# ScalarE copies the turned tile ahead of its exponentials, and two one-number activations stand where tables are to come in

## What is computed

```python
def diff_attention(q, k, v, lam):
    ...
        s = jnp.einsum("bhcqd,bhckd->bhcqk", qb, kf) * (dh ** -0.5)
        a = jax.nn.softmax(s, axis=-1)
        return jnp.einsum("bhqk,bhkd->bhqd", a[:, :, 0] - lam * a[:, :, 1], vf)
def mixer_c(...):
    o = diff_attention(q, k, v, lam)
    o = rms_norm(o, subln, LN_EPS) * (1.0 - lambda_init)
    return o.reshape(B, S, C_MIX).astype(x.dtype) @ w_out
```

## Time and profile before

| | us |
|---|---|
| median of 3 runs | 2598.41 |
| lowest, highest | 2597.32, 2599.71 |
| the profiled execution, its own time | 2594.23 |
| its span (first to last instruction) | 2592.4 |
| TensorE busy in the span | 2473.3 (95%) |
| VectorE busy | 1169.7 (45%) |
| ScalarE busy | 688.6 (27%) |
| GpSimd busy | 1898.8 (73%) |
| mean granted clock of TensorE | 0.979 |

### The profile page before, as it was taken

The page is one execution under the profiler, slowest core; times in us unless marked ns, Lnnn a source line. Parts: engine busy times, 40 slices in busy tenths (PEclk is TensorE's granted clock), DMA queues, the critical chain, the costliest instruction groups (busy, mean ns, idle before and its releaser), DMA issues.

```text
span 2592.4 us, 32309 instructions
## 1 busy us (share of the span) xinstructions
PE 2473.3 (95%) x11170; PEld 1897.2 (73%) x11170; DVE 1169.7 (45%) x1541; ACT 688.6 (27%) x1244; POOL 1898.8 (73%) x1537
## 2 busy tenths in 40 slices
PE   7988989999989989999999999999999999999998
PEld 6745668888867853668888777866888878678886
DVE  7485463331061677463330176445423565553323
ACT  2264333330021138133330023145110131450101
POOL 8803368888867953678888778844999898449996
PEclk9989999999999999999999999899999999999999
DMA  4201012222212210112222223211222222112222
GB/s 170 89 1 41 33 65 98 96 97 97 98 63 94 94 51 1 61 66 96 94 96 97 89 72 107 86 58 41 98 98 97 89 98 81 49 50 101 93 97 90
DMA packets 57544, 207.08 MB, mean 80 GB/s; under 512 B 6512, under 2 KB 6896, under 8 KB 57200
## 3 DMA queue, kind: packets, MB, share of 16 engines
q1 hardware_dynamic: 55872, 199.87, 21.9%
q10 hardware_dynamic: 1584, 5.96, 0.6%
HBM read 203.71 MB, written 2.10 MB: 79 GB/s over the span
## 4 chain that ended last, share of the span: by engine, by line
PE 79%; DVE 11%; POOL 4%; issue 3%; ACT 2%; DMA 0%; POOLq 0%; DVEq 0%; ACTq 0%; SPq 0%
PE bank L696 22%; PE bank L697 21%; PE bank L698 21%; PE bank L771 3%; PE bank L726 3%; POOL w_hi L2322 2%; PE bank L820 2%; PE bank L799 2%; POOL w_lo L2325 2%; DVE region L1754 1%; PE bank L885 1%; DVE branch_lo L1734 1%; DVE moving_lo L1959 1%; PE bank L841 1%; DVE x L1968 1%
## 5 line engine op out<-in xcount | busy, mean ns | idle before, releaser
L2322 POOL TENSOR_TENSOR w_hi<-ring,unit 128x512 fp32r<-128x512 f32 x750 | 843.6, 1125 | 554.6 <-PE bank L698 417.1
L2325 POOL TENSOR_TENSOR w_lo<-ring,w_hi 128x512 fp32r<-128x512 f32 x750 | 1032.8, 1377 | 58.8
L696 PE MATMUL bank<-moving_hi,w_hi 128*128 128x512 f32 x1962 | 777.8, 396 | 29.9 <-DVE moving_lo L1959 18.8
L697 PE MATMUL bank<-moving_lo,w_hi 128*128 128x512 f32 x1962 | 771.6, 393 | 0.0
L698 PE MATMUL bank<-moving_hi,w_lo 128*128 128x512 f32 x1962 | 770.4, 393 | 0.0
L696 PEld LDWEIGHTS bank<-moving_hi,w_hi 128*128 128x128 f32 x1962 | 372.0, 190 | 125.0 <-issue 25.8
L698 PEld LDWEIGHTS bank<-moving_hi,w_lo 128*128 128x128 f32 x1962 | 372.6, 190 | 78.9
L697 PEld LDWEIGHTS bank<-moving_lo,w_hi 128*128 128x128 f32 x1962 | 372.6, 190 | 76.7 <-issue 1.2
L2269 DVE TENSOR_TENSOR region<-region,bank 128x512 f32<-128x512 f32 x64 | 39.7, 681 | 278.4 <-PE bank L698 278.4
L1941 DVE SCALAR_TENSOR_TENSOR region<-x,bank 128x512 f32<-128x512 f32 x32 | 21.3, 686 | 284.6 <-PE bank L698 284.5
L771 PE MATMUL bank<-region 64*128 64x512 f32 (+3 forms) x448 | 130.5, 601 | 15.6 <-DVE region L1728 4.4
(11 more groups left out here) (271 smaller groups left out, 3477.4 us busy)
## 6 DMA issues: line engine op xcount, KB each, us to landing
ring<-in_weights SPq DMA_DIRECT2D x375, 512.0 KB, 3.2
x<-in_x_t ACTq DMA_DIRECT2D x4, 512.0 KB, 8.4
out<-region SPq DMA_DIRECT2D x8, 256.0 KB, 2.2
region<-in_tables ACTq DMA_DIRECT2D x1, 1312.0 KB, 6.6
region<-in_tables ACTq DMA_DIRECT2D x1, 1024.0 KB, 5.6
region<-in_p_t ACTq DMA_DIRECT2D x2, 512.0 KB, 4.8
region<-in_tables SPq DMA_DIRECT2D x1, 320.0 KB, 10.1
small_w<-in_small_w ACTq DMA_DIRECT2D x1, 320.0 KB, 6.0
```

Of the source, the lines that this page charges most:

```text
L696: pe.matmul(bank, lhs[0], rhs[0], start=start, stop=False, skip_group_check=True)
L697: pe.matmul(bank, lhs[0], rhs[1], start=False, stop=False, skip_group_check=True)
L2322: pool.tensor_tensor(w_parts[0][:, s, at], ring[:, s, at], unit[:, 0:1].broadcast_to([P, BLK // 2]), ALU.mult).then_inc(split_hi, 1)
L2325: pool.tensor_tensor(w_parts[1][:, s, at], ring[:, s, at], w_parts[0][:, s, at].bitcast(F32), ALU.subtract).then_inc(split_ready, 1)
```

## The change

Three edits in ScalarE's `attention_c`. The copy of turn n-3 is issued ahead of the two exponentials of turn n instead of behind them. An exponential of one number for each partition (the constant of the layer norm) is issued ahead of the loop, and a root of the same number behind the loop, ahead of the last three copies; both write to `table_in`, a new tile of two numbers that nobody reads. The new tile lies behind `unit`, so the tiles allocated after it move by its size.

```diff
         unit = sb("unit", [P, 1])
+        table_in = sb("table_in", [P, 2])
...
+                act.activation(table_in[:, 0:1], col("eps_ln"), ACT.Exp)
                 for n, (u, i) in enumerate(turns):
                     t = TURN_AT[(u, i)]
                     act.wait_ge(turned, max(t - 2, first_c))
+                    if n >= 3:
+                        copy_turned(*turns[n - 3])
                     for c in range(2):
                         act.wait_ge(maxed, 2 * t + c + 1)
                         at = 2 * (t % 4) + c
                         act.activation(blend_slot(t, c), psum[2 * (t % 2) + c], ACT.Exp, bias=negmax[:, at:at + 1],
                                        accum_out=rowsum[:, at:at + 1]).then_inc(exped, 1)
-                    if n >= 3:
-                        copy_turned(*turns[n - 3])
                     if i == 3 and n > 2 * ST:
                         finish(units[n // ST - 2])
+                act.activation(table_in[:, 1:2], col("eps_ln"), ACT.Sqrt)
                 for at in turns[-3:]:
                     copy_turned(*at)
```

## The result

| | before | after |
|---|---|---|
| median of 6 runs | 2598.26 | 2587.41 us |
| lowest, highest | 2597.26, 2599.71 | 2586.96, 2591.98 us |
| profiled execution, its span | 2594.23, 2592.4 | 2587.32, 2585.5 us |

The ratio of after to before is 0.9961, with a 95% interval from 0.9948 to 0.9974. The change gains 10.9 us between the medians and 6.9 between the profiled executions. The forecast was 6.0 (a ratio of 0.9977, above that interval); the stage came out nearly as worked, and the whole did not. The two profiled executions also differ where nothing was changed: the stage starts at 945.10 before and at 942.80 after, so of their 6.9 us 2.3 lie ahead of it, and 1.9 are lost again behind it. What the change does to the stage is therefore read from distances inside it.

The account below looks back on a forecast made before the run. TensorE, holding 79% of the span, was taken as the bound, with stalls and two table loads on its path in the subtracted softmaxes. 1.28 + 3.48 + 1.28 = 6.04 us takes 2598.41 to 2592.4; range 2590.2 to 2595.8.

Parts of the forecast that it names:

- Step 1: Start of the subtracted softmaxes: the added exponential moves its table load into ScalarE's idle time; gain 1.28 us, hidden price 0.
- the clock's 0.5 to 0.6: Second scores: less TensorE standing may keep the clock up, 0.60 us more, total 6.6; kept inside the forecast's 0.74.
- Step 2: Softmax loop: copy ahead of exponentials removes the 0.58 us stall of each unit's first value matmul; gain 3.48 us.
- Six stalls, not seven: Seven value matmuls waited for the copy, the last after the last scores; six count, 6 x 0.58 = 3.48 us.
- The exponentials late by ScalarE at a unit's border: Behind finish and copy, exponentials start 0.43 us late; 0.64 us of slack remains, so the cost is 0.
- Step 3: End of the softmaxes: the root added ahead of the last three copies takes its table load off the chain; gain 1.28 us.
- the last turning was not late: The copy it needs, delayed by the added root, would still end in time, with 0.29 us to spare.
- Squares brought no other load: Copies and squares run under the root's table; squares needing another table would bring the load back, but they don't.
- A load costs more than its bar: Rival: each load also holds up its surroundings, making the tables worth double; 8.7 us in total, 2589.7, chance 0.02.
- The stage's 6.04: Forecast gain in the subtracted softmaxes of heads_c: 1.28 + 3.48 + 1.28 = 6.04 us.
- the shift passes on unchanged: Everything after the softmaxes waits through TensorE, so the full gain reaches the end: median 2598.41 becomes 2592.4 us.
- dips of the clock behind the stage: Later clock dips, lying in time and not in the program, hit busier or idler TensorE: up to 1 us either way.

Follow-up runs that it names:

- e3: Kernel before plus both added activations (early exponential and early root) with their tile, copy order unchanged: ratio 0.9982, stage 94.71 us.
- e4: Kernel before plus only the early added exponential with its tile, no added root, copy order unchanged: ratio 0.9993, stage 96.06 us.
- e7: Kernel before with only the copy of each unit's last turn moved ahead of the exponentials, no added activation: loop 60.21 us against 63.96.
- e8: Kernel before with the other three of four copies moved ahead, each unit's last turn's copy left behind the exponentials: loop 63.96 us.
- e6: Kernel before plus only the early added root with its tile: ratio 0.9992, stage 96.40 us.
- e15: Kernel before, unchanged, one more profiled execution: stage 97.39 us, span 2593.8 us.
- e1: Kernel before, unchanged, profiled once more: ratio 1.0001, stage 97.85 us, span 2591.7 us.
- e11: Changed kernel without its early exponential (order and root only): ratio 0.9970, stage 94.18 us.
- e13: Changed kernel without its early root (order and exponential only): ratio 0.9961, stage 92.62 us.
- e14: Changed kernel, run a third time unchanged: ratio 0.9959, stage 91.24 us.
- e9: Kernel before plus six unread 128 x 512 matmuls after the sums of squares, in TensorE's gap ahead of the roots: ratio 1.0003.

## Why the prediction was wrong

1. *Step 1, the exponential's table.* Right in place and direction. The load lies in the idle time (936.59), the second scores start 5.01 us after the first (942.80, 947.81) in place of 6.29, exactly the 1.28. What I left to a rival, the clock's 0.5 to 0.6, came in e3 and e4 whole (against the first profile of before) and in the changed kernel for about 0.1; against the mean of the four profiles of before, for nothing.

2. *Step 2, the order.* Right, and e7 and e8 show the cause alone. Six stalls, not seven, were on the path. The term was 3.48 and measured 3.75: five boundaries give 0.59 each, the first gives 0.78, since the next maxima there come 2.56 us behind the last ones instead of 3.34. The exponentials late by ScalarE at a unit's border (984.76) cost nothing, as worked; they were late by 0.26 us, and not by 0.43. From the first scores to the last value matmul the stage is 5.1 us shorter (6.49 - 1.36) where 4.8 was forecast.

3. *Step 3, the root's table.* Right: 1.36 for 1.28, and the last turning was not late. The copy that the last turning needs started at 1025.94 and was done by 1026.5, 0.8 us ahead of that turning (1027.32), where I had worked out 0.29. Squares brought no other load.

4. *A load costs more than its bar.* That rival is out: hiding the root's load gained 1.36 us (e6), its bar's 1.28 and 0.08, and the stage gained 6.5 and not 8.7. The Trainium skill (ScalarE: Activation LUTs, "What ACT_TABLE_LOAD costs") would have had 2.66 for a switch; the traces here don't agree.

5. *The sum and the range.* Here the prediction failed. The stage's 6.04 measured 6.49 (91.35 against 97.84). Put on the 2598.41 that I started from, that is 2591.9, inside the range; the measured 2587.41 is 4.5 lower. The failed step is the sentence that the shift passes on unchanged from the profiled execution to the median, with a spread of 1.2 us. Its three runs did not show how executions of this kernel spread. Over all comparisons, 101 executions of before have a mean of 2597.1 and a standard deviation of 2.5 us, 19 of the changed kernel 2588.3 and 1.5. Those means are 8.85 apart. So of the 10.9 us, 6.3 are the stage's in the mean of the profiles (6.5 in the first two); 8.85 - 6.3 = 2.5 are the change's too, in the means, and not in the stage; and 10.85 - 8.85 = 2.0 are the luck of six executions against six (1.1 by those of before lying above their mean, 0.9 by those of after below theirs). The comparisons were not all made on one chip, and taken one by one they give 10.1, 9.1, 10.0 and, with five executions only, 7.6; weighted by their executions 9.4, which would leave 1.4 to luck.

6. *What the 2.5 are.* The clock on record with each execution gives about half. Its mean over the span is 0.9776 in the 95 executions of before that have it and 0.9787 in the 19 of the changed kernel, and among executions with the same recorded clock (0.977 to 0.980, to three digits) the two kernels are 7.0 to 8.1 us apart, 7.5 by a fit over all. So some 1.3 us go with a lower clock in the executions of before. About 0.4 of this is the clock behind the gap ahead of the roots (e15 against e1). I had written of it in the wrong direction: dips of the clock behind the stage were noise to me, up to 1 us either way, lying in time and not in the program, while the gap of step 3 itself has a part in one of them, and others move with the program (the low stretch at 1112 to 1118 of before, 0.53, stands at 1104 to 1110 of the changed kernel, 0.50). For the rest, 7.5 - 6.3 = 1.2, I have no cause that the runs show; with a standard error of 0.4 on the 7.5 and on the 8.85 alike, it is uncertain by about 0.8, and it stays open. The parts measured over the whole (order 2.6 to 3.3, exponential 1.2 to 1.4, root 2.3 to 2.6, between medians and between means) add up to 6.1 to 7.3, and the profiled spans are 7.1 apart in the means of four and five.

   The profiles of e11 and e13 take 1556.9 and 1556.4 us behind the stage, 5 or more above the changed kernel in any of its five. Some 4 of these lie in one stretch, over a thousand microseconds behind the stage. From the same VectorE instruction to the same, this stretch takes 95.4 to 95.7 us in the five profiles of the changed kernel, 99.7 in e13 and 99.4 in e11. The changed kernel, then e13:

```profile
2111.00:2206.50 95.50, 88.82 (x448) 73.97 (x446) 37.02 (x48) 13.17 (x25) 80.60 (x64) 0.93 0.26 90
```

```profile
2114.00:2214.00 100.00, 91.46 (x449) 76.36 (x447) 35.75 (x48) 13.26 (x25) 79.29 (x64) 0.90 0.26 86
```

   The clock is granted at 0.90 there, in e11 too, in place of 0.91 to 0.95 in the five. But the one with 0.91 (e14) is only 0.3 us longer there than the others. So it can be told where these executions lose their time; that a lower clock is the whole of it, and why it falls there in these, is not shown.

The chances: faster by over 0.2% was the likeliest case, at 0.68, and it came. The low end of the range lay 2.8 us above the measured time.

## What to carry to other kernels

A step that stands behind another on an in-order engine for no reason of its own is worth moving only where someone on the path waits for it: here one copy in four carried the whole 3.75 us, and the other three nothing. The table loads of this stage started only when the waits of their activations were over (948.60, after 9.88 us without work; 1040.93, right behind the last square), so their 1.28 us lay on the path where these activations did; a throwaway activation of one element per partition, without a wait, moved each into an earlier place off the path for 0.2 us. And before a gain of a few tenths of a per cent is forecast to the microsecond, the spread of single executions must be known; a gap on TensorE that is made shorter can also be worth more than its length (0.4 us more on average here).

## What the runs showed of the hardware

- After TensorE had waited about 2.7 us (2.64 to 2.74), the granted clock was low behind the wait in 6 of 10 profiles of the same instructions; after 1.36 us, in none of 9. The sixteen records of the spreading took 8.83 us with the low clock at their start and 7.13 at full clock.
- Executions of one kernel with a lower mean granted clock took longer: before, 2594.3 us on average at 0.980 and 2599.7 at 0.976.
- The first turns of the stage ran at a granted clock of 0.52 for 17 us in one profile (e11), which cost 1.5 us.
- An activation of one element for each partition took 0.20 us, for the exponential and the root alike; each load 1.28, with the next instruction 0.01 to 0.02 us behind.
- A matmul of 128 x 512 in fp32 has two records in the trace and took 0.9 us (e9: six in 5.42 us).
